# One read of the modulation weights for two conditioning vectors, and a new table of places for the modulation blocks

## The reference

```python
silu_c = jax.nn.silu(c)
silu_cc = jax.nn.silu(c_ctx)
for i in range(DEPTH_2):
    mod_l = (silu_c @ ada_w[i] + ada_b[i])[:, None, :]
    mod_c = silu_cc @ ada_w[i] + ada_b[i]
    sh1_l, sc1_l, g1_l, sh2_l, sc2_l, g2_l = jnp.split(mod_l, 6, axis=-1)
    sh1_c, sc1_c, g1_c, sh2_c, sc2_c, g2_c = jnp.split(mod_c, 6, axis=-1)
    h_l = rms_norm_2(x, norm1_g[i]) * (1.0 + sc1_l) + sh1_l
    h_c = rms_norm_2(ctx, norm1_g[i]) * (1.0 + sc1_c) + sh1_c
```

## Time and profile before

| | |
|---|---|
| median of three runs | 2078.06 us (2073.74 to 2079.80) |
| profiled execution: its time | 2079.8 us |
| profiled execution: span in the profile | 2077.8 us, clock 0.99 |
| TensorE busy | 2016.8 us (97%) |
| VectorE busy | 1709.8 us (82%) |
| ScalarE busy | 1256.9 us (60%) |
| bytes read from memory | 585.89 MB |

### The profile page before, as it was taken

The page is one execution under the profiler, slowest core; times in us unless marked ns, Lnnn a source line. Parts: engine busy times, 40 slices in busy tenths (PEclk is TensorE's granted clock), DMA queues, the critical chain, the costliest instruction groups (busy, mean ns, idle before and its releaser), DMA issues.

```text
span 2077.8 us, 30715 instructions
## 1 busy us (share of the span) xinstructions
PE 2016.8 (97%) x12645; PEld 1803.1 (87%) x12645; DVE 1709.8 (82%) x1882; ACT 1256.9 (60%) x1269; POOL 39.5 (2%) x77
## 2 busy tenths in 40 slices
PE   4999999999899999999999999999999999999998
PEld 4899899999888899999888888888888888888886
DVE  6687887989777758887458898898888988888887
ACT  3468744655334454443347777777777777777775
POOL 3010000000000000000000000000000000000000
PEclk9999999999999999999999999999999999999999
DMA  9874676868743439999439999999999999999994
GB/s 319 258 251 139 195 245 206 259 224 266 243 162 113 152 121 337 310 305 307 156 134 358 370 351 364 350 363 358 359 362 351 367 355 358 358 356 363 361 370 160
DMA packets 337568, 589.03 MB, mean 283 GB/s; under 512 B 10517, under 2 KB 150315, under 8 KB 337424
## 3 DMA queue, kind: packets, MB, share of 16 engines
q1 hardware_dynamic: 333776, 580.70, 80.1%
q0 software_dynamic: 3008, 5.78, 1.0%
q10 hardware_dynamic: 640, 0.52, 0.1%
HBM read 585.89 MB, written 1.07 MB: 282 GB/s over the span
## 4 chain that ended last, share of the span: by engine, by line
PE 91%; DVE 5%; ACT 2%; issue 1%; DMA 0%; SPq 0%; DVEq 0%; ACTq 0%
PE bk L650 15%; PE bk L652 15%; PE bk L651 15%; PE bk L644 12%; PE bk L645 11%; PE bk L646 11%; PE bk L721 1%; PE bk L1179 1%; DVE wlo L1926 1%; DVE macc L1951 1%; PE bk L706 1%; PE bk L708 1%; PE bk L707 1%; ACT whi L1316 1%; PE bk L1228 1%
## 5 line engine op out<-in xcount | busy, mean ns | idle before, releaser
L1926 DVE TENSOR_TENSOR wlo<-raw,whi 128x2048 fp32r<-128x2048 f32 x477 | 1081.1, 2268 | 235.1 <-ACT whi L1316 234.2
L1316 ACT CAST whi<-raw 128x2048 fp32r<-128x2048 f32 x477 | 903.1, 1894 | 382.8 <-PE bk L652 259.0
L644 PE MATMUL bk<-HH,whi 128*128 128x256 f32 x1480 | 428.3, 289 | 7.9 <-DVE HL L1997 6.6
L645 PE MATMUL bk<-HL,whi 128*128 128x256 f32 x1480 | 420.6, 284 | 0.0
L646 PE MATMUL bk<-HH,wlo 128*128 128x256 f32 x1480 | 420.3, 284 | 0.0
L650 PE MATMUL bk<-whi,xh 128*128 128x512 f32 x896 | 354.7, 396 | 0.0
L652 PE MATMUL bk<-wlo,xh 128*128 128x512 f32 x896 | 349.4, 390 | 0.0
L651 PE MATMUL bk<-whi,xl 128*128 128x512 f32 x896 | 348.8, 389 | 0.0
L644 PEld LDWEIGHTS bk<-HH,whi 128*128 128x128 f32 x1480 | 286.0, 193 | 12.7 <-issue 8.4
L645 PEld LDWEIGHTS bk<-HL,whi 128*128 128x128 f32 x1480 | 286.1, 193 | 1.1 <-issue 0.7
L646 PEld LDWEIGHTS bk<-HH,wlo 128*128 128x128 f32 x1480 | 285.8, 193 | 0.0
(11 more groups left out here) (376 smaller groups left out, 2489.5 us busy)
## 6 DMA issues: line engine op xcount, KB each, us to landing
raw<-in_moe_w SPq DMA_DIRECT2D x334, 1024.0 KB, 6.0
raw<-in_ada_w SPq DMA_DIRECT2D x56, 1024.0 KB, 5.4
raw<-in_ff_w SPq DMA_DIRECT2D x40, 1024.0 KB, 5.7
raw<-in_w_in SPq DMA_DIRECT2D x29, 1024.0 KB, 5.4
raw<-in_w_mod SPq DMA_DIRECT2D x24, 1024.0 KB, 5.4
raw<-in_w_up SPq DMA_DIRECT2D x22, 1024.0 KB, 5.1
raw<-in_attn_w_qkv SPq DMA_DIRECT2D x12, 1024.0 KB, 6.1
raw<-in_w_branch SPq DMA_DIRECT2D x8, 1024.0 KB, 5.0
```

Of the source, the lines that this page charges most:

```text
L644: pe.matmul(o, sh, mh, start=start, stop=False, skip_group_check=True)
L645: pe.matmul(o, sh, ml, start=False, stop=False, skip_group_check=True)
L1316: act.copy(whi[k][:, :n], raw[q.slot[i]][:, :n]).then_inc(q.hi_done.mark(g), 1)
L1926: dve.tensor_tensor(wlo[k][:, :n], raw[q.slot[i]][:, :n], whi[k][:, :n].bitcast(F), ALU.subtract).then_inc(q.taken.mark(i), 1)
```

## The change

The context's four groups (2, 0) to (2, 3) are no longer loaded. The M slabs of (1, 0) to (1, 3) are read once and VectorE runs its four instructions on each of them twice, first with the tokens' vector into one `macc`, then with the context's into the next; only the last instruction marks the buffer taken. Both groups are summed at the same place. The DMA list is eight slabs of 1 MB shorter (the plan has 72 M slabs in place of 80), and VectorE and TensorE keep their numbers of instructions for the modulation. The rest of the table is new: groups stand at other slots, and the last four of matrix 3 are all summed at "x4". Two calls that no longer find work are gone, and the coefficient of `h3` is computed before the projection's residuals.

```diff
-                 ((0, 8), (9, 10), 12), ((2, 0), (21, 22), 25), ((2, 1), (24, 26), 28), ((0, 9), (29, 31), 33),
+                 ((0, 8), (9, 10), 12), ((1, 0), (21, 22), 25), ((0, 9), (29, 31), 33), ((1, 1), (24, 26), "x1"),
...
+        mplan += [((3, i), (95 + 3 * i, 97 + 3 * i), 99 + 3 * i) for i in range(8)]
+        mplan += [((3, 8), (120, 121), "x4"), ((3, 9), (122, 123), "x4"), ((3, 10), (124, 125), "x4"), ((3, 11), (126, 127), "x4")]
...
             mlist.append((which, g, when))
+            if which == 1 and g < 4:
+                mlist.append((2, g, when))
...
-                yield from pe_mods(A_T, 86.5 + c - 1)
...
+                dests = [which] + ([2] if which == 1 and g < 4 else [])
+                for d in dests:
+                    n = mnum[d, g]
+                    acc = macc[n % 4]
+                    if k0 == 0 and n >= 4:
+                        dve.wait_ge(*(yield from B.full("mod", n - 4)))
+                    for j in range(4):
+                        sc = csil[:, mcol[d] + k0 * 4 + j:mcol[d] + k0 * 4 + j + 1]
...
+                        if j == 3 and d == dests[-1]:
+                            t.then_inc(st.taken.mark(i), 1)
...
-                    yield from dve_mods(88.5)
-                    yield from dve_coeff("h3", 32, "n20", 1, 8)
```

More of the change, by code:

```diff
@@ L378, in build @@
         mplan = [((0, 4), (0, 1), 3), ((0, 5), (2, 3), 5), ((0, 6), (4, 5), 7), ((0, 7), (6, 7), 9),
[5 rows of a table removed]
[L384 to L387, removed]
[4 rows of a table added]
+        mplan += [((3, i), (95 + 3 * i, 97 + 3 * i), 99 + 3 * i) for i in range(8)]
+        mplan += [((3, 8), (120, 121), "x4"), ((3, 9), (122, 123), "x4"), ((3, 10), (124, 125), "x4"), ((3, 11), (126, 127), "x4")]
+        mats = {0: wmod, 1: ada[0], 3: ada[1]}
         at_slot = {}
@@ L439, in build @@
             mlist.append((which, g, when))
+            if which == 1 and g < 4:
+                mlist.append((2, g, when))
         last_slab = {(t[0], t[1]): i for i, (kind, t, *_) in enumerate(st.plan) if kind == "M" and t[2] == 1}
-        mlist = [(m[0], m[1], last_slab[m[0], m[1]], m[-1]) for m in mlist]
+        mlist = [(m[0], m[1], last_slab[min(m[0], 1) if m[0] == 2 else m[0], m[1]], m[-1]) for m in mlist]
         mnum = {(d, g): n for n, (d, g, *_) in enumerate(mlist)}
@@ L1940, in dve_mslabs @@
                 v = raw[st.slot[i]][:, :].rearrange("p (k n) -> p k n", k=4)
[L1941 to L1957, removed]
+                dests = [which] + ([2] if which == 1 and g < 4 else [])
[6 more added lines that the diff above has]
+                        sc = csil[:, mcol[d] + k0 * 4 + j:mcol[d] + k0 * 4 + j + 1]
+                        if k0 == 0 and j == 0:
+                            t = dve.tensor_scalar(acc[:, :], v[:, 0, :], sc, None, ALU.mult)
+                        else:
+                            dve.wait_ge(*acc_told[d])
+                            t = dve.scalar_tensor_tensor(out=acc[:, :], in0=v[:, j, :], scalar=sc, in1=acc[:, :], op0=ALU.mult, op1=ALU.add)
+                        if j == 3 and d == dests[-1]:
+                            t.then_inc(st.taken.mark(i), 1)
+                            acc_told[d] = st.taken.now()
+                        else:
+                            t.then_inc(dve_step.mark("acc"), 1)
+                            acc_told[d] = dve_step.now()
         bm = [0]
@@ L2281, in dve_branches @@
                     yield from dve_lo(st, 37 + c + NP)
-                    yield from dve_mslabs(st.gi[38 + c + NP])
             yield from dve_mods(40.5)
@@ L2429, in dve_attention @@
             yield from dve_mods(86)
+            yield from dve_coeff("h3", 32, "n20", 1, 8)
             for c in range(4):
                 if c == 3:
-                    yield from dve_mods(88.5)
-                    yield from dve_coeff("h3", 32, "n20", 1, 8)
                     yield from dve_squares("x3")
```

## The result

The changed kernel takes 2087.72 us (median of five runs, 2085.89 to 2091.49), the kernel before 2078.06 in the same rounds (2073.73 to 2079.80): ratio 1.0051, 95% interval 1.0039 to 1.0063. It is slower by 9.7 us. The forecast was 2079.4, within 2069 to 2088, and most likely no change; 2087.72 lies just inside that wide range, but on the side that I held less likely.

A forecast was written before the change was run, and what follows sets the result against it. TensorE, busy 97%, was taken as the bound, with VectorE almost a second one in the first half. Terms +5.2 + 6.1 + 1.6 - 4.4 - 3.4 - 3.8 = +1.3 us took 2078.06 to 2079.4, range 2069 to 2088.

The forecast's parts named there:

- slots 21 to 24: Extra VectorE passes ahead of the last attention rows: TensorE waits 3.8 us plus a slow spell of 1.4, +5.2 us.
- slots 42 to 48: Eight VectorE passes where three stood make a split late: 5.4 us idle plus 0.7 for a slow spell, +6.1 us.
- second residual: TensorE's 6.43 us wait for squares shrinks as VectorE passes ahead of it go: -4.4 us, bounds -2.85 and -5.7.
- attention: Slot 77's sum leaves with its 1.66 us bank wait and slow spell, slot 85's pass goes: -3.4 us.
- Rival (a): VectorE stays the bound through the feed-forward, TensorE late by four passes, 11.9 us for 6.1: 2085.2 us, chance 0.27.
- Slots 120 to 127: Eight M slabs in a row at 334 GB/s outrun the lead of the halves: +1.6 us, bounds 0 and 6.0.
- Fourth residual: Three sums move into TensorE's idle gap, saving 2.4 us, and the slow spell goes, 1.4: -3.8 us.
- The sum of clock terms in the forecast: Slow spells: 1.4 added at slots 21 to 24, 0.7 at 42 to 48; 1.4 removed at attention and 1.4 at fourth residual.
- Rival (b): Crowded places mostly absorbed: second and third cost nothing, the first only its idle 3.8 us; 2070.3 us, chance 0.18.
- (c): Memory is the bound, and 8.4 MB less at 356 GB/s give 23.6 us: 2054.5 us, chance 0.02.
- the signs that I had named as refuting the forecast: First two waits (near 245, and 385 to 425 us) missing or twice as large, or second residual still waiting 6 us.

The follow-up runs named there:

- twelve_spread: Changed kernel with the same twelve VectorE passes of slots 42 to 62 spread to other places in that stage: 2084.79 us, ratio 1.0036 to the kernel before.
- sums_between_slabs: `places_mended_ten_slots` with the sums of (3, 8) to (3, 10) put back between slabs, only (3, 11) at x4: 2072.86 us, ratio 0.9975 to the kernel before.
- places_mended_ten_slots: Changed kernel with doubled slabs at 24, 26, 33, 37, 45, 48, 51, 54, single groups re-placed, last eight M slabs in ten slots: 2069.76 us, 0.9961.
- ten_slots: Changed kernel with the last eight M slabs in ten slots as before, all still summed at x4: 2084.75 us, ratio 1.0037 to the kernel before.
- spread: Changed kernel with doubled slabs at 24, 26, 28, 37, 42, 47, 51, 56 and single ones at 21, 22, 31, 33, 38, 39: 2087.19 us, ratio 1.0053.
- single_at_21: Changed kernel with single group (0, 9) at slots 21, 22 and doubled groups at 24, 26, 29, 31: 2089.89 us, ratio 1.0051 to the kernel before.

## Why the forecast was wrong

The prediction's terms beside the time that TensorE lost or regained between the same slabs, against the first trace of before, in the three traces of the changed kernel (to about 0.1 us):

| step | forecast | traces |
|---|---|---|
| slots 21 to 24 | +5.2 | +4.6, +6.2, +6.1 |
| slots 42 to 48 (with the sums at x1 and slot 63) | +6.1 | +8.9, +10.3, +12.0 |
| second residual | -4.4 | -6.8, -6.7, -5.3 |
| attention | -3.4 | -2.4, -2.4, -2.5 |
| from slot 107 to the fourth residual: 120 to 127, and sums | -2.2 | +0.9, -1.6, +1.1 |
| sum | +1.3 | +5.2, +5.8, +11.4 |

**Slots 21 to 24: right.** The wait was 3.70 us (forecast 3.8), and the slow stretch behind it came in two of three traces, at 1.5 us (forecast 1.4). The rest of the row, 0.9, is one sum more.

**Slots 42 to 48: the step that failed.** It was put at 6.1 us and measured 8.9, 10.3 and 12.0. The idle part was right: 4.8 us (forecast 5.4), if the wait for ScalarE's squares is counted with those for halves; these alone are 3.9, 2.4 and 2.4. Two parts of it were not. I took the sums that TensorE does there as "taken from elsewhere"; with the one at x1 they are 2.7 us by 0.9 a set (the 0.79 of the earlier trace rows was low), and they come back only behind the stage, in terms that I had costed without them. And I wrote that "a slow spell while VectorE is the bound costs nothing, only the last may, so I add 0.7". The traces have one, two and two stretches here, 3.4, 6.8 and 10.2 us of half clock, which is 1.5, 3.0 and 4.5 us in place of 0.7. Rival (a) came out near the measured size by another road. VectorE did not stay the bound: behind slot 48 it regained its lead, as forecast, and TensorE is full there, in the first trace of after

```profile
427.00:510.00 83.00, 83.00 (x685) 82.67 (x685) 75.06 (x104) 46.65 (x55) 0.00 (x0) 1.00 0.72 233
```

and, being full, keeps what it has lost. Taken with the second residual the idle time did not grow at all: 0 + 6.4 us before, 4.8 + 1.6 after, 2.2 + 4.2 in `twelve_spread`. What these two rows cost together, 2.1, 3.6 and 6.7 us where the forecast has 1.7, differs from trace to trace by the clock alone.

**Second residual: right in kind, too small.** The wait fell to 1.59 (forecast 2.1), and two of the three traces lie beyond the bound of -5.7. What I left out is the stretch of 6.8 us at half clock at 554 us in the trace of before, behind which nothing of that length stands in the first two traces of after; the third has one of 3.4 us, and gains 1.4 less.

**Attention: too large, since another wait came.** The wait of 1.66 went, but TensorE waits 1.84 for VectorE's `sr` at 614.26. It is not a new pass that makes `sr` late: one stood at slot 76 before too (3.11 us, from 600.61). TensorE, no longer held at the bank nor slowed behind it, now reaches the wait for `sr` before VectorE has it; this is read from the two timelines and was not tried by itself. The other two bank waits grew from 1.05 to 1.93 us, 0.9 in place of the 0.5 forecast. What the row gains is the stretch at 605 us and the sum that left.

**Slots 120 to 127: right in kind.** Waits of 2.34, 1.46 and 2.24 us for a half near 989 (forecast 1.6), all in the range up to 6.0. ScalarE's copy stands behind a load there:

```profile
985.04 1.91 ACT L1315 CAST whi<-raw 128x2048 fp32r<-128x2048 f32 x1 [2.45 <-DMA raw<-in_ff_w]
```

The queue moved 337 GB/s in the stretch. The Trainium skill, "DMA: Bandwidth & Descriptors", Specifications, has 358 GB/s as the limit for one core. With it the forecast's estimate for this row was 0, no wait; the experts come near it with 356, this stretch does not.

**Fourth residual: the gap was filled, the slow stretch stayed.** Without the waits near 989 the last row is -1.4, -3.1 and -1.1 us, in place of -3.8. The idle 2.24 is gone in all three, and `sums_between_slabs` shows that the term can reach its size, 3.1 us in the medians and 3.8 in the traces. But "with nothing idle the slow spell there should go as well" failed: the second trace has one of 3.4 us there, as before, and the other two have one of 6.8, from 1012.03 in the first, in the third

```profile
1020.97:1027.79 6.82, 6.82 (x25) 6.10 (x25) 2.10 (x9) 1.76 (x5) 0.00 (x0) 0.50 0.44 152
```

In `places_mended_ten_slots`, where the four sets stand in the same gap, there is none; in `ten_slots`, which has them there too and no wait near 989, there is one of 6.8. What brings it stays open.

**The clock.** The sum of clock terms in the forecast was -0.7 us, fewer slow stretches after than before. By the mean clock of all executions it was about +4. The error is not that I took a wrong length for one, but that I treated the stretches of one trace as fixed parts of the kernel: I removed those I saw and charged new ones sparingly, while each new idle piece can have one behind it in some executions. None of the signs that I had named as refuting the forecast appeared, since all of them were about idle time. That idleness causes the stretches is argued from where they stand and from their going with the waits; it was not tried by giving TensorE other work in the same gap.

Rival (b) and (c) are out. (c) most clearly: it had 2054.5, and with 8.4 MB less the kernel is slower. In the fastest version too the gain is in TensorE's waits and clock.

## What to carry to other kernels

On an engine that is 97% full, a table of places is judged stage by stage: count the passes of the second busiest engine in each stage, then the room between them, and look at every piece of work queued behind the new place (a bank to be freed, squares, a split). Work that is saved elsewhere does not pay for a stage that is over its room. And where the granted clock changes from trace to trace, read two or three traces of the same kernel before charging or crediting a slow stretch; here the idle time was worth about 4 us and the clock, on average, about as much.

## What the runs showed of the hardware

Stretches of TensorE at 0.50, the 1.2 GHz level, stand at other places in each execution of one program: in the spans of the three traces of the changed kernel 40.6, 48.2 and 57.6 us in all. Most are 3.4 or 6.8 us long; `spread` and `single_at_21` have one of 10.2. One of 3.4 us in full work costs 1.5 us. The same 3.70 us of idle time was followed by one in two of three traces. That is a part of why one program's executions spread over 7 to 9 us: of the kernel before, the 25 executions with a mean clock of 0.990 took 2079.6 us on average and the 25 with 0.991 took 2076.2. It is not all: the eight with 0.988 took 2078.6. What else differs was not looked into, beyond that slot 2 ended at 69.9 to 73.3 us in the five traces of the two kernels.
